# A different order for the opening: weight halves, x tiles and turns in a PE-bound encoder step

## The reference, cut to what matters

```python
def rms_norm(x, g):
    xf = x.astype(jnp.float32)
    y = xf * lax.rsqrt(jnp.mean(xf * xf, axis=-1, keepdims=True) + EPS)
    return (y * g.astype(jnp.float32)).astype(x.dtype)

def swiglu(h, w_gate, w_up, w_down):
    return (jax.nn.silu(h @ w_gate) * (h @ w_up)) @ w_down
...
        x = x + 0.5 * swiglu(rms_norm(x, norm_g[layer, 0]), ffn_w_gate[layer, 0], ffn_w_up[layer, 0], ffn_w_down[layer, 0])
```

## Time and profile before

| what | value |
|---|---|
| median of 3 runs | 2036.04 us |
| the 3 runs | 2035.72, 2036.04, 2039.59 us |
| the profiled execution, its time | 2037.71 us |
| the same, span from the first to the last instruction | 2035.7 us |
| PE busy (share of the span) | 2024.1 us (99%) |
| DVE, ACT, POOL busy | 1436.3, 809.8, 662.7 us |
| mean granted TensorE clock | 0.998 |

### The profile page before, as it was taken

How to read it: one execution, slowest core, us unless ns; L and a number is a source line. 1 busy time by engine, 2 the same in 40 slices (tenths; PEclk the granted TensorE clock), 3 DMA queues, 4 the chain that set the end, 5 groups by cost and what they waited for, 6 DMA issues and landing times.

```text
span 2035.7 us, 34452 instructions
## 1 busy us (share of the span) xinstructions
PE 2024.1 (99%) x13790; PEld 2003.3 (98%) x13790; DVE 1436.3 (71%) x2280; ACT 809.8 (40%) x1354; POOL 662.7 (33%) x723
## 2 busy tenths in 40 slices
PE   9999999999999999999999999999999999999998
PEld 8999999999899999999999999999999999999998
DVE  5786675874766678667587688485777878576675
ACT  6343333453344434333345344242335444333343
POOL 2562442402000056244240354262421356243330
PEclk9999999999999999999999999999999999999999
DMA  6233232333222223323233123223242213323222
GB/s 167 71 90 82 73 92 68 94 96 80 62 65 64 68 65 91 82 79 84 71 101 100 52 71 98 76 71 88 71 130 65 75 46 84 96 71 94 73 58 83
DMA packets 312846, 165.23 MB, mean 81 GB/s; under 512 B 15539, under 2 KB 310271, under 8 KB 312688
## 3 DMA queue, kind: packets, MB, share of 16 engines
q1 hardware_dynamic: 307840, 157.31, 28.2%
q0 software_dynamic: 2672, 4.65, 1.0%
q10 hardware_dynamic: 2176, 1.07, 0.2%
HBM read 159.01 MB, written 4.00 MB: 80 GB/s over the span
## 4 chain that ended last, share of the span: by engine, by line
PE 96%; DVE 2%; ACT 1%; issue 0%; DMA 0%; SPq 0%; DVEq 0%; ACTq 0%
PE psum L537 31%; PE psum L538 31%; PE psum L539 31%; PE psum L910 1%; PE psum L579 0%; PE psum L596 0%; ACT probs L1244 0%; DVE in_lo L1380 0%; DVE conv_y L1816 0%; DVE probs_both L1742 0%; DMA x_nat<-in_x_prompt 0%; PE psum L807 0%; PE psum L544 0%; DVE stats L1729 0%; DVE probs L1714 0%
## 5 line engine op out<-in xcount | busy, mean ns | idle before, releaser
L537 PE MATMUL psum<-xg_hi,in_hi 128*128 128x320 f32 x1952 | 610.2, 313 | 1.8 <-DVE in_lo L1380 0.9
L539 PE MATMUL psum<-xg_hi,in_lo 128*128 128x320 f32 x1952 | 603.2, 309 | 0.0
L538 PE MATMUL psum<-xg_lo,in_hi 128*128 128x320 f32 x1952 | 603.1, 309 | 0.0
L1899 POOL TENSOR_TENSOR sums<-in_raw 128x256 f32<-128x256 f32 x288 | 268.0, 951 | 695.6 <-DVE in_lo L1392 468.4
L537 PE MATMUL psum<-f_hi,f_out_hi 128*128 128x320 f32 x1408 | 435.9, 310 | 0.0
L539 PE MATMUL psum<-f_hi,f_out_lo 128*128 128x320 f32 x1408 | 435.1, 309 | 0.0
L538 PE MATMUL psum<-f_lo,f_out_hi 128*128 128x320 f32 x1408 | 435.1, 309 | 0.0
L537 PEld LDWEIGHTS psum<-xg_hi,in_hi 128*128 128x128 f32 x1952 | 366.4, 188 | 6.1 <-issue 1.7
L538 PEld LDWEIGHTS psum<-xg_lo,in_hi 128*128 128x128 f32 x1952 | 366.5, 188 | 0.9
L539 PEld LDWEIGHTS psum<-xg_hi,in_lo 128*128 128x128 f32 x1952 | 366.4, 188 | 0.0
L537 PE MATMUL psum<-mix_hi,in_hi 128*128 128x320 f32 x864 | 267.0, 309 | 0.0
(11 more groups left out here) (233 smaller groups left out, 2771.6 us busy)
## 6 DMA issues: line engine op xcount, KB each, us to landing
in_raw<-in_ffn_w_gate SPq DMA_DIRECT2D x87, 512.0 KB, 4.1
in_raw<-in_ffn_w_up SPq DMA_DIRECT2D x86, 512.0 KB, 5.4
out_raw<-in_ffn_w_down SPq DMA_DIRECT2D x96, 384.0 KB, 3.4
out_raw<-in_ffn_w_down SPq DMA_DIRECT2D x32, 256.0 KB, 3.0
in_raw<-in_mix_w_in SPq DMA_DIRECT2D x14, 512.0 KB, 4.6
out<-y_nat SPq DMA_DIRECT2D x5, 512.0 KB, 3.2
in_raw<-in_mix_w_in SPq DMA_DIRECT2D x8, 256.0 KB, 4.4
out_raw<-in_mix_w_out SPq DMA_DIRECT2D x16, 128.0 KB, 3.1
```

The lines of the kernel that those rows point to most:

```text
L537: pe.matmul(dst, w_hi, v_hi, start=first, stop=False)
L538: pe.matmul(dst, w_hi, v_lo, start=False, stop=False)
L539: return pe.matmul(dst, w_lo, v_hi, start=False, stop=last)
L1899: last = pool.tensor_tensor(to[:, part], a[:, part], b[:, part], op)
```

## The change

Four things are changed, all in the opening.

1. ACT no longer issues the halves b=1 of the first weights right behind the halves b=0. It now waits until the halves b=0 have landed (`first_landed`), and issues the two transfers then, ahead of its first work on them.
2. On ACT the high part of w_gate's first half comes ahead of that of x tile 0, and w_up's ahead of x tile 1. `start_tile(2)` moves ahead of the wait for the halves b=1, and `start_high(3)` between the two high parts of those halves. DVE's order follows it.
3. In `first_unit` PE turns tiles two at a time: tiles 2 and 3 ahead of k=1, 4 and 5 ahead of k=3, 6 and 7 ahead of k=5.
4. The turns of the second half of x, and the small transposes and waits that stand ahead of the first of them, come one k later: ahead of every odd k.

```diff
             def first_unit():
                 for k in range(KT):
-                    if 1 <= k < 7:
-                        if k in (1, 3):
+                    if k in (1, 3, 5):
+                        if k < 5:
                             pe.wait_ge(start_landed[1 + k // 2], 16 * 3)
                         turn_x(k + 1)
+                        turn_x(k + 2)
                     pe.wait_ge(xg_lo_done, k + 1)
...
                     if q == 1:
-                        if (t, k) == (0, 0):
+                        if (t, k) == (0, 1):
                             pe.wait_ge(start_landed[3], 16 * 3)
...
-                        if k % 2 == 0:
+                        if k % 2 == 1:
                             turn_x(8 + 4 * t + k // 2)
...
             act.dma_start(norm_nat[:, :], norm_g.rearrange("l n (k c) -> (l n k) c", c=P)).then_inc(norm_landed, 16)
-            for b in range(2):
+            def load_first(b):
+
                 for t, w in enumerate((w_gate, w_up)):
                     act.dma_start(in_raw[:, 0, t, 4 * b:4 * b + 4],
                                   w[0, 0].rearrange("(k p) c -> p k c", p=P)[:, 4 * b:4 * b + 4, 0:P]).then_inc(in_landed[0] if b else first_landed, 16)
+
+            load_first(0)
...
             act.wait_ge(vec_ready, 1)
+
+            act.wait_ge(first_landed, 32)
+            load_first(1)
+            first_hi(0, 0)
             start_high(0)
+            first_hi(1, 0)
             start_high(1)
-            act.wait_ge(first_landed, 32)
-            first_hi(0, 0)
-            first_hi(1, 0)
             start_copy(0)
             start_copy(1)
+            start_tile(2)
             act.wait_ge(in_landed[0], landed(0))
             first_hi(0, 1)
-            start_tile(2)
+            start_high(3)
             first_hi(1, 1)
-            start_high(3)
             square(0, 0, 0, P, 0)
...
             dve.wait_ge(vec_ready, 1)
+            first_low(0, 0)
             start_low(0)
+            first_low(1, 0)
             start_low(1)
-            first_low(0, 0)
-            first_low(1, 0)
+            start_low(2)
             first_low(0, 1)
-            start_low(2)
+            start_low(3)
             first_low(1, 1)
-            start_low(3)
             start_keep(3)
```

## The result

| | kernel before | changed kernel |
|---|---|---|
| median of 20 runs | 2036.16 us | 2042.24 us |
| lowest and highest | 2035.37, 2039.59 | 2038.10, 2045.20 |
| profiled execution, time and span | 2037.71, 2035.7 | 2044.91, 2043.1 |

The change makes the kernel 6.1 us slower. The ratio is 1.0028, with a 95% interval of 1.0021 to 1.0035 (4.3 to 7.1 us), so it is just outside the 0.2% (4.1 us) that I called the least measurable difference. The runs also scatter more: over 7.1 us instead of 4.2.

A forecast was written before the change was run, and what follows sets the result against it. PE was taken as the bound, busy 2024.1 of 2035.7 us. Start +0.08, returns saved -0.3, waits +1.3 against 0.78 before: +0.3 us, so a median of 2036.3, range 2035.2 to 2038.6.

The forecast's parts named there:

- the second halves landing late: Weight halves b=1 in the opening: landing costs nothing up to 12.15 us, one to one beyond; k=4 starts at 16.35.
- L: Time at which the weights' late halves b=1 land: taken as 12.7 us, between bounds of 11.5 and 16.4.
- late halves: Rival: the two late transfers share the wires with SP's and land at 16.4; about +4.0 us, 2040.0; chance 0.13.
- The two transfers on ACT: ACT's two issues, now from 6.35 to 7.4 us, delay the first highs: gives away 1.05 us.
- the issues are held up: Rival: ACT's two issues are held like SP's, so ACT and the first product start 2.2 us late; 2038.2; chance 0.08.
- The first product: PE starts k=0 at 9.45 us against 9.37 and ends it at 10.6 instead of 10.5.
- The turns in pairs: PE's turns of x in the first unit: three returns fewer save 0.3 us; k=2 waits 0.2, starting at 12.85.
- k=3 at L+2.1: PE's k=3 in the first unit can start 2.1 us after the late halves land; without a wait, at 14.85.
- The clock: Rival: six small transposes with waits around them in the opening lower PE's clock, worth 1.7 us; 2037.9; chance 0.05.
- The end of the unit: From k=4 on, 5.2 us with waits of 0.15 and 0.3 at k=6 and k=7: end at 21.5 against 21.2.
- The shift by one k, the queues of SP and POOL: Later turns of x's second half, SP's third weight load 0.8 us later, POOL's bias transfers: all cost nothing.
- A rule weighed: Skill's transfer estimate, 2.0 us plus bytes over 436 GB/s: 2.6 us, landing near 9.5, change -0.2 us; not followed.

The follow-up runs named there:

- the fillers: The changed kernel with 40, then 14, useless matmuls ahead of PE's wait at k=3: 2044.82 us, then 2043.87 us against 2043.58 for the changed kernel.
- the kernel with the issue at 4 us: The changed kernel, but ACT issues the halves b=1 without waiting for the first halves' landing: 2035.93 us, ratio 1.0001 to the kernel before.

## Why the prediction was wrong

I forecast +0.3 us, 0.95 for no measurable change and 0.04 for slower; it is +6.1. The failed step is *the second halves landing late*: L, taken as 12.7 with 16.4 as the upper bound, was 18.65. The mechanism was in the text as the rival *late halves*, with 0.13, and its price per microsecond of L was about right; its size was cut off at a bound that was none.

- *The two transfers on ACT.* Right. First halves landed at 6.56 (forecast 6.3), issues at 6.64 and 7.11 of 0.44 and 0.53 us, first high at 7.69 (7.4). The rival *the issues are held up* fell: ACT was never held at issuing.
- *The first product.* 9.71 (forecast 9.45); all of the difference comes from the later landing. *The turns in pairs*: k=2 started at 12.93 (12.85), and the pairs alone make no difference that the medians can tell.
- *L.* I took it from the lengths of other transfers, issue to landing, and asked which of them looked most like it. But these lengths are mostly time in line. SP's second weights were issued at 5.5, 6.1 and 6.75, the first two ahead of both of ACT's, and holding all three and piece 3 back took 7.0 us off w_up's landing, holding piece 3 alone 3.8. I had counted 512 KB at half of the rate "from about 8 on", that is, an equal share from the first moment; ACT's queue had none until 11.0. The rows of before fit the order of issue too: w_gate, w_up, their second halves and x's pieces landed in nearly the order in which they were issued, whichever queue they were on. I read them as queue against queue.
- *The bound of 9.5 us* came from a transfer of SP's own queue, where piece 3 stood behind it in the same queue (landings 17.1 and 17.9). ACT's late half had piece 3 in the other queue, beside its last packets, and that added 3.8 us of tail. Before, SP was itself held at issuing and sent piece 3 at 9.6; with ACT's transfers out of the way it sent it at 7.45, into the late halves' tail. That part of the change, what SP would issue sooner, I did not follow.
- *k=3 at L+2.1.* Right: 20.54 for L = 18.65. The formula gives 18.65 - 12.15 - 0.3 = +6.2 us for this L, against an estimated 5.9 in the profiled execution without the clock. That the median is 6.1 too is partly luck: it mixes executions with other landings and with the cost of the clock in them.
- *The clock* was a rival by itself, with 0.05, and it came in addition: some 1.5 us in the profiled execution by the estimate above. Two terms that I had priced apart come together. The clock fell in each trace here in which PE waited as long as this (5.47, 6.42 and 4.74 us). But a long wait isn't needed: it also fell behind 2.58, 1.69, 1.55 and 0.69 us, and it did not behind 1.47 us in the kernel with only the late issue. What brings it is left open; the fillers fit idle time as the cause and don't prove it.
- *The end of the unit.* Close: forecast 5.2 us from k=4 to the last product; it is 6.2 (22.31 to 28.5), 1.2 of them the lower clock.
- *The shift by one k, the queues of SP and POOL.* Right in that they cost nothing that can be seen: the shift alone changes nothing, and the difference of the spans is that of the opening. SP's load of the third pair came at 21.1, not at the forecast 15.2, and even that is not seen behind the opening.
- *A rule weighed.* The estimate of 2.6 us for such a transfer was still further off than the rows: 7.4 and 11.5 us were measured.

The Trainium skill, DMA: Bandwidth & Descriptors, section Queues, rings and completion order, says that a DMA engine takes turns between the queues that have work for it, a packet at a time. From 12.5 to 13.5 us the trace agrees in the counts (287 and 293 packets). From 7.6 to 11 it does not show it (1475 and none), with ACT's transfers long issued. That one descriptor generator works off the issues of both engines in order would fit both stretches; this is argued, not shown. What is shown is that work issued ahead on the other queue delays the first packets, and that the last packets of a transfer can be held up by what is issued after it. Why the tail comes is open.

The scatter of the changed kernel's runs, 2038.1 to 2045.2, fits a landing that varies (18.65 and 17.8 in two profiles) with or without the lower clock behind it; I have not split it further.

## What to carry to other kernels

In this opening a transfer's time from issue to landing was mostly its place in line, and the line was common to both issuing engines. To bound a transfer that is moved, sum the bytes that both queues have issued ahead of its new moment: that bounds its start. Its end depends also on what is issued just behind it. Here holding an issue back to leave the wires to another was safe only ahead of the big block of the other queue: at 4 us it cost nothing in the median, at 6.6 it cost 6 us, because SP had put most of its 1 MB of second weights into the line in between. And where a wait is put into an engine's fixed order, price what stands behind it (here a tile of x that had nothing to do with the late weights), at a landing time that may be double the one you believe in.

## What the runs showed of the hardware that I had not expected

- Issued work of one queue can move no packet for almost 4 us (issue of w_gate's half done at 7.1, none up to 11) while the other queue's earlier issues are served; later both move about equally (287 and 293 packets from 12.5 to 13.5).
- The last 0.02 MB of a transfer took 3.6 us while the other queue was busy: 56 packets came through in 2 us beside 171 large ones (3.6 KB each), and in the kernel with the issue at 4 us the last 93 (0.04 MB) needed 2 us beside 987 small ones. With piece 3 held back there was no such tail, and with the second weights held to 8.1 us hardly one (2 packets after 11.0).
- The issue itself told nothing of this: 0.44 and 0.53 us, like the first two at 1.2 and 1.7 us (0.45 and 0.53).
- The first halves' landing, issued at 1.2 and 1.7 us with the same work around, came at 6.3 to 6.6 in most profiles and at 8.0 in one.
- The granted clock can fall behind short waits of PE: in the kernel with the issue at 4 us behind one of 0.69 and one of 0.32 us (0.59 from 16 to 18, 0.50 from 18 to 22), with the stretch ahead of them at 1.00.
